# A hybrid decoder step on one core: the gated recurrence goes tile by tile, the first tile ahead of the shared block and the other three inside it

## What is computed

```python
mod = silu(c) @ w_ada + b_ada                    # shift, scale, gate, twice
z = (x * (1 + scale1) + shift1) @ w_in           # 8004 columns, split among the branches
logf = log(lb + (1 - lb) * sigmoid(fa))          # lb from lb_param
# branch A, 8 heads, state S of 128x128, in chunks of 32 tokens (4 for the samples):
bcum = cumsum(logf); k = -expm1(logf)
qe, ke, kd = silu(qa) * exp(bcum), k * exp(-bcum), k * exp(bcum[last] - bcum)
o = qe @ S + mask(qe @ ke.T) @ v                 # v = ia
S = exp(bcum[last]) * S + kd.T @ v
oa = o * rsqrt(mean(o**2) + 1e-6) * a_gnorm * silu(ga)
# branch B: indexer -> top-k keys -> grouped attention with a T5 bias -> ob
x = LN1(ALPHA * x + gate1 * ((sigmoid(gate_a) * oa + sigmoid(gate_b) * ob) @ w_out))
x = LN2(ALPHA * x + gate2 * PEER(x * (1 + scale2) + shift2))   # 8 heads x 16 experts a token
```

## Time and profile before

| | |
|---|---|
| median of three executions | 2604.06 us |
| the profiled execution's own time | 2610.84 us |
| its span, first to last instruction | 2608.9 us |
| mean granted TensorE clock | 0.829 |
| busy: TensorE, VectorE, ACT, POOL | 1945.3, 1459.8, 578.5, 655.6 us |
| moved by DMA | 794.7 MB, mean 305 GB/s |
| stages 1 and 2, stage 3, beat -1, beats 0 to 272 | 393, 222, 202, 1792 us (about) |

### The profile page before, as it was taken

The page is one execution under the profiler, slowest core; times in us unless marked ns, Lnnn a source line. Parts: engine busy times, 40 slices in busy tenths (PEclk is TensorE's granted clock), DMA queues, the critical chain, the costliest instruction groups (busy, mean ns, idle before and its releaser), DMA issues.

```text
span 2608.9 us, 26429 instructions
## 1 busy us (share of the span) xinstructions
PE 1945.3 (75%) x8372; PEld 1048.6 (40%) x8372; DVE 1459.8 (56%) x2984; ACT 578.5 (22%) x1902; POOL 655.6 (25%) x610
## 2 busy tenths in 40 slices
PE   4999994885898986975567756577646667979666
PEld 1878532554664433441243422234311223536311
DVE  1000107563472536689856899747954997353654
ACT  1000002111013544212422223312221113121221
POOL 0000003220002233323333333333433323332342
PEclk8999996675799998787789977889867778695779
DMA  8357301123657989999999999999999999999797
GB/s 315 124 184 279 126 20 50 43 69 124 186 169 279 387 321 371 413 385 361 344 398 420 394 415 374 355 374 418 403 368 346 394 385 409 404 405 366 285 421 301
DMA packets 203327, 794.69 MB, mean 305 GB/s; under 512 B 24435, under 2 KB 87763, under 8 KB 130230
## 3 DMA queue, kind: packets, MB, share of 16 engines
q0 software_dynamic: 81280, 589.48, 56.6%
q1 hardware_dynamic: 116358, 185.59, 20.7%
q10 hardware_dynamic: 5552, 17.94, 2.3%
HBM read 771.24 MB, written 23.91 MB: 305 GB/s over the span
## 4 chain that ended last, share of the span: by engine, by line
PE 25%; DMA 20%; DVE 18%; issue 9%; SPq 3%; ACT 1%; POOL 0%; ACTq 0%; another core or an unknown queue 0%; DVEq 0%; POOLq 0%
DMA uv<-in_peer_uv,eidr 14%; PE PS L1249 9%; PE PS L1296 7%; PE PS L1367 4%; DVE uv L1656 3%; DVE m L1686 2%; DMA uv<-in_peer_uv,eids 2%; DVE sels L1687 2%; SPq L1155 1%; PE PS L1319 1%; PE PS L1419 1%; DMA vec<-mod_d 1%; PE PS L1334 1%; DMA qbt<-mix_d 1%; SPq L1149 1%
## 5 line engine op out<-in xcount | busy, mean ns | idle before, releaser
L1249 PE MATMUL PS<-uv,dg 128*32 128x512 f32 x2176 | 731.3, 753 | 397.0 <-ACT dg L1512 362.9
L1656 DVE CUSTOM_DVE_ANT_0 uv<-uv,h2r 128x1024 f32<-128x1024 f32 x544 | 666.8, 1226 | 416.0 <-DMA uv<-in_peer_uv,eidr 326.9
L1216 POOL DMA_INDIRECT uv<-in_peer_uv,eidr x512 | 552.6, 1079 | 1366.8 <-PE PS L1249 1037.3
L1249 PEld LDWEIGHTS PS<-uv,dg 128*32 128x32 f32 x2176 | 193.4, 127 | 799.3 <-ACT dg L1512 496.4
L1500 ACT ACTIVATE acts<-dots 128x2 f32<-128x2 f32 x272 | 55.3, 203 | 1085.5 <-DVE dots L1656 1048.9
L1367 PEld LDWEIGHTS PS<-h2T,wr 128*128 128x128 f32 x1280 | 178.2, 223 | 63.7 <-issue 60.1
L1367 PE MATMUL PS<-h2T,wr 128*128 128x128 f32 (+1 forms) x1280 | 189.5, 308 | 1.1 <-ACT h2T L1586 1.1
L1296 PE MATMUL PS<-htb,wr 128*128 128x416 f32 x512 | 186.5, 520 | 0.0
L417 PE MATMUL PS<-hT,wb 128*128 128x272 f32 (+1 forms) x608 | 143.7, 398 | 14.4 <-PEq L134 14.4
L1512 ACT ACTIVATE dg<-fold,wts 128x32 f32<-128x32 f32 x544 | 140.9, 306 | 0.0
L417 PEld LDWEIGHTS PS<-hT,wb 128*128 128x128 f32 (+1 forms) x608 | 114.5, 189 | 46.2 <-issue 20.8
(11 more groups left out here) (281 smaller groups left out, 2066.6 us busy)
## 6 DMA issues: line engine op xcount, KB each, us to landing
wr<-in_w_oq SPq DMA_DIRECT2D x120, 512.0 KB
wb<-in_w_in SPq DMA_DIRECT2D x15, 2048.0 KB, 10.2
w_ada_p<-in_w_ada POOLq DMA_DIRECT2D x16, 1024.0 KB, 8.1
wr<-in_w_late SPq DMA_DIRECT2D x32, 512.0 KB
w_ada_b<-in_w_ada SPq DMA_DIRECT2D x8, 1024.0 KB, 20.7
h2r<-h_d ACTq DMA_DIRECT2D x32, 256.0 KB
uv<-in_peer_uv,eidr POOLq DMA_INDIRECT x512
kvr<-in_cache_kt SPq DMA_DIRECT2D x48, 128.0 KB
```

Source lines behind the costliest of these rows:

```text
L1216: nc.gpsimd.indirect_dma_start(out=uv[j % RING][:, :], out_offset=None, in_=table, in_offset=bass.IndirectOffsetOnAxis(ids, 0)).then_inc(e ...
L1249: mm = nc.tensor.matmul(PS[ST * g:ST * g + ST, at:at + 512], dg[:, j % DR, :], uv[j % RING][:, D + 512 * half:D + 512 * half + 512], start ...
L1656: c.step(nc.vector.tensor_tensor_reduce(out=uv[j % RING][:, 0:D], in0=uv[j % RING][:, 0:D], in1=h2r[:, q // HT % 2, g % 2, :], scale=1.0, ...
```

## The change

The recurrence is written once as a set of functions (`recurrence`) over a half of the heads (four) and one tile of 128 tokens, with buffers of 24 KB per partition. Stage 3 does only tile 0, as two halves, and the sample. It spills q, the gate and v of tiles 1 to 3 to memory (rec_d, recv_d) and the states after tile 0 (carry_d). In the shared block each tile has two halves of six steps, ("rec", n, k), put from beats 0, 42 and 96 on at 1.2 a beat: 0 ACT loads (inputs, states and a mask), 1 logarithms, scan and scaling, 2 scores and transposes, 3 products and state steps, 4 outputs, states stored, squares, 5 mean square, inverse root, norm. The result is written straight into mgt, which SP no longer loads for tiles 1 to 3. Their buffers lie over the attention's (tile 1 from selp on, tiles 2 and 3 from gbt on), so that late weights use three of the six ring buffers in these beats, and tile 1's indexer and top-k start at beat 10 instead of 0. The products of a chunk are taken from the 32 rows of the chunk, four narrow ones per head in place of one wide one with a zeroed operand; vc and POOL's work for it are gone. The sample's elementwise work is done for all heads at once. The parameters (lbm, gn, eps6, cmask, meanm) are loaded and computed in stage 1. Shortened, the diff is:

```diff
@@ stage 1
+            for j in range(2):
+                pool.dma_start(lbp[:, j, :], dap(a["lb_param"], j * D, [[1, P], [P, H]]), ...).then_inc(m_lbd, 16)
+            act.wait_ge(m_sm, 1)
+            nc.scalar.activation(lbm[:, 0:2, :], lbp[:, :, :], ACT.Exp).then_inc(m_lb, 1)
@@ stage 3
+        def exponents(act, n):
+            b = buf(n)
+            act.wait_ge(r["scan"], n + 1)
+            nc.scalar.activation(b.eb[:, :], b.bc[:, :], ACT.Exp).then_inc(r["exp"], 1)
+            nc.scalar.activation(b.ke[:, :], b.bc[:, :], ACT.Exp, scale=-1.0).then_inc(r["exp"], 1)
+            act.wait_ge(r["d"], n + 1)
+            nc.scalar.activation(b.ab[:, :], b.ab[:, :], ACT.Exp).then_inc(r["ed"], 1)
...
+        def states(dve, c, n, k):
+            b = buf(n)
+            dve.wait_ge(r["ds"], 4 * n + k + 1)
+            for i in range(4):
...
+                    c.step(nc.vector.scalar_tensor_tensor(b.st[k + 1][:, i, :], b.st[k][:, i, :], b.eb[:, at:at + 1], ds, ALU.mult, ALU.add), done)
...
+        def products(pe, n, first=0, end=4):
+            b = buf(n)
+            for k in range(first, end):
+                lo = CH * k
...
+                for i in range(4):
+                    last = nc.tensor.matmul(bank(banks(n)[k % 2], P, P, P * i), b.kd[lo:lo + CH, i, :], b.v[lo:lo + CH, P * i:P * i + P],
+                                            start=True, stop=True)
+                last.then_inc(r["ds"], 1)
...
-                    nc.tensor.matmul(bank(2 + t % 2), kd_t[:, h % 2, t, :], vc[:, t, :, :], start=True, stop=True).then_inc(r_ds, 1)
...
+            for t in range(1, TILES):
+                for j, src in enumerate((q_s, sn_s)):
+                    sp.dma_start(dap(rec_d, (2 * (t - 1) + j) * P * H * P, [[H * P, P], [P, H], [1, P]]), src[:, :, P * t:P * t + P]).then_inc(r_spill, 16)
+                sp.dma_start(dap(recv_d, (t - 1) * P * D, [[D, P], [1, D]]), v_s[:, t, :]).then_inc(r_spill, 16)
@@ TensorE's order in stage 3
+            rec.scores(pe, 0)
+            rec.scores(pe, 1)
+            rec.products(pe, 0, 0, 2)
+            ... (scores and transposes of the sample)
+            rec.products(pe, 0, 2, 4)
+            rec.products(pe, 1)
+            ... (outputs, mean squares; states and outputs of the sample, head by head)
@@ shared block, the beats
-    for t, b in ((1, 0), (2, 52), (3, 106)):
+    for t, b in ((1, 10), (2, 52), (3, 106)):
         ix, tp, ys, qs = tile_steps(t)
+        put(b - 10, 1.2, *[("rec", n, k) for n in (2 * t - 2, 2 * t - 1) for k in range(6)])
...
-        nxt = (nxt + 1) % WRING
+        nxt = (nxt + 1) % (WRING if n < len(early_w) or piece[0] != "late" else WRING // 2)
@@ SP
-                mixed(mgt[:, :, :], 0, t, z_ga)
+                if t == 0:
+                    mixed(mgt[:, :, :], 0, t, z_ga)
...
+                    if 1 <= t < TILES:
+                        sp.wait_ge(r["mg"], 2 * t)
+                        sp.wait_ge(r_cst, 16 * 2 * t)
@@ ACT
+            def recur(n, k):
+                t, g, b = rec_tile(n), n % 2, rec_buf(n)
+                if k == 0:
+                    if n >= 1:
+                        act.wait_ge(r["mg"], n)
+                        act.wait_ge(r_cst, 16 * n)
...
+                    if g == 0:
+                        act.dma_start(b.keep[:, :], dap(a["keep"], 0, [[N, P], [1, 512]])).then_inc(r_ld, 16)
+                    for j, dst in enumerate((b.q, b.sn)):
+                        act.dma_start(dst, dap(rec_d, (2 * (t - 1) + j) * P * H * P + 512 * g, [[H * P, P], [1, 512]])).then_inc(r_ld, 16)
+                    act.dma_start(b.v, dap(recv_d, (t - 1) * P * D + 512 * g, [[D, P], [1, 512]])).then_inc(r_ld, 16)
+                    act.dma_start(b.st[0][:, :, :], dap(carry_d, 512 * g, [[H * P, P], [1, 512]])).then_inc(r_ld, 16)
+                elif k == 1:
+                    act.wait_ge(r_ld, ld_at(n))
+                    rec.logs(act, n)
+                    rec.exponents(act, n)
...
@@ VectorE
+                if kind == "rec" and k == 1:
+                    dve.wait_ge(r_ld, ld_at(t))
+                    rec.decay(dve, c, t)
+                    rec.scaled(dve, c, t)
+                elif kind == "rec" and k == 2:
+                    rec.masked(dve, c, t)
+                elif kind == "rec" and k == 3:
+                    for i in range(4):
+                        rec.states(dve, c, t, i)
+                elif kind == "rec" and k == 5:
...
+                    rec.normed(dve, c, t)
@@ TensorE
+                elif kind == "rec" and k == 2:
...
+                    rec.scores(pe, t)
+                elif kind == "rec" and k == 3:
+                    rec.products(pe, t)
+                elif kind == "rec" and k == 4:
+                    rec.outputs(pe, t)
+                elif kind == "rec" and k == 5:
+                    rec.mean_squares(pe, t)
```

More of the change, by code:

```diff
@@ L12 @@
 import math
+from dataclasses import dataclass
 from contextlib import ExitStack
@@ new lines, in _ @@
+            last.then_inc(q_ln, 1)
+            rec.exponents(act, 0)
+            rec.exponents(act, 1)
+            act.wait_ge(q_scan, 1)
+            nc.scalar.activation(ebS[:, :], bcS[:, :], ACT.Exp).then_inc(q_exp, 1)
+            nc.scalar.activation(keS[:, :], bcS[:, :], ACT.Exp, scale=-1.0).then_inc(q_exp, 1)
+            act.wait_ge(q_d, 1)
+            nc.scalar.activation(abS[:, :], abS[:, :], ACT.Exp).then_inc(q_ed, 1)
+            rec.keys_out(act, 0)
+            rec.keys_out(act, 1)
@@ new lines, in _ @@
+            act.wait_ge(q_kdp, 1)
+            nc.scalar.activation(kdS[:, :, :], PS[0:ST, 512 * 5:512 * 7].rearrange("p (h k) -> p h k", k=P), ACT.Copy).then_inc(q_kdt, 1)
+            for n in range(2):
+                rec.squares(act, n)
+                rec.inverse_root(act, n)
+            act.wait_ge(q_o, H)
+            nc.scalar.activation(bcS[:, :], bank(7, H * ST), ACT.Square).then_inc(q_sq, 1)
+            act.wait_ge(q_ms, 1)
+            nc.scalar.activation(keS[:, :], bank(7, H * ST, P, 256), ACT.Ln, bias=eps6[:, 0:1]).then_inc(q_lnms, 1)
@@ L630, in _ @@
+            act.wait_ge(q_lnms, 1)
+            nc.scalar.activation(keS[:, :], keS[:, :], ACT.Exp, scale=-0.5).then_inc(q_rstd, 1)
         @block.vector
@@ new lines, in _ @@
+            for i in range(4):
+                rec.states(dve, c, 0, i)
+            dve.wait_ge(q_kdp, 1)
+            c.step(nc.vector.tensor_tensor(by_head(scmS[:, :]), by_head(bank(4, H * ST, ST)), smask[:, :].unsqueeze(1).to_broadcast([ST, H, ST]), ALU.mult), q_scm)
+            for i in range(4):
+                rec.states(dve, c, 1, i)
+            for h in range(H):
+                sample(h)
+                if h in (1, 3):
+                    rec.normed(dve, c, h // 2)
+            dve.wait_ge(q_rstd, 1)
@@ L766, in _ @@
                                             start=False, stop=b == NB - 1)
-                last.then_inc(r_o, 1)
-            mean_squares(H - 1)
+                last.then_inc(q_o, 1)
+            rec.outputs(pe, 0)
+            sample_states(0)
+            sample_outputs(0)
+            rec.mean_squares(pe, 0)
+            rec.outputs(pe, 1)
+            sample_states(1)
+            sample_outputs(1)
+            rec.mean_squares(pe, 1)
+            for h in range(2, H):
+                sample_states(h)
+                sample_outputs(h)
@@ L868, in program @@
     x1 = zu("x1", [P, D])
+    assert zu_at[0] - where["z"] - rest == REC_BYTES
     h2 = zu("h2", [P, D])
@@ L875, in program @@
     assert zu_at[0] <= where["z"] + 65536
+    assert where["z"] + 65536 - at_selp >= REC_BYTES
+    late_half = [rec_buffers("e1", at_selp)]
+    rest_half = [rec_buffers("e2", where["z"] + rest)]
+    keep_of = {1: late_half[0].keep, 2: rest_half[0].keep}
     zb, zb_at = over("z", rest)
@@ L1035, in program @@
                 if kind in ("y", "late") or kind == "query" and k < 2 * PH]
+    early_w = [s for s in beats[-1] if s[0] in ("y", "late") or s[0] == "query" and s[2] < 2 * PH]
     use_at, slot_at, nth_at, before = {}, {}, {}, {}
@@ L1038, in program @@
     for n, piece in enumerate(pieces_w):
[L1039 removed]
+        if piece[0] == "y" and piece[2] == 0 or n == len(early_w):
             nxt = 0
```

533 lines of the change are left out of this document (301 added, 232 removed).

## The result

The changed kernel takes 2676.26 us (median of 4 runs, 2670.14 to 2678.89), the kernel before 2608.16 in the same session. The ratio is 1.0265, 95% interval 1.0235 to 1.0296: slower by 68 us.

What follows compares the result with a forecast made beforehand. TensorE and VectorE alternate in the stage; the block is bound by TensorE for 18 beats, then gathers, with VectorE second. -128 + 72 + 49 + 55 = +48 on 2604 gave 2652 us, range 2555 to 2700.

Steps and rivals of the forecast that it cites:

- The stage, -128: Recurrence stage ahead of the block: without three tiles it takes 94 us against 221.6, saving 128 us (110 to 140).
- C: Tile 1 and stage: TensorE's clock falls to 1.2 GHz after waits, costing 20 and 18 us; 2690 us, chance 0.12.
- D: Recurrence stage: hardly shorter, 130 us, because sample products are short and many; saving 92, total 2688 us, chance 0.07.
- Parameters in stage 1, at nothing: First stage: takes over some 5 us of parameter arithmetic at no cost, up to 15 us if a load lands late.
- Tile 1, +72: Beats 0 to 10, on TensorE's path: waits 52, work 27, less some 7 us of present idle, adding 72 us.
- Tiles 2 and 3, +49 and +55: Beats 42 to 52 and 96 to 106, VectorE's path: work and waits, less 15 us won back each, plus traffic.
- Rival B: Loads in the block are short, 6.5 and 5.2 us instead of 15 and 12: +2, 2606 us, chance 0.17.
- At nothing: Shared block: three weight slots, tile 1's later index and top-k, SP's new waits and carry stores cost nothing.
- The rule on the queues: ACT's loads in the block: 94 or 75 GB/s by trace, though round-robin might let two busy queues share evenly.
- The rule on table switches: ACT in the six halves: 1.28 us per table load by trace; 2.66 with a drain would add 33 us.
- What would show it: Stage 85 to 105 us, beats 0 to 18 some 210, six load waits of 10 or more, DMA share under 0.8.
- Ring covers stalls (A): Shared block: the gather ring absorbs every stall, three tiles cost 39 us: -89, 2515 us, chance 0.17.

Runs made afterwards that it cites:

- experiment 1: The changed kernel without the recurrence of tiles 1 to 3, tile 0's result stored in its place, so only the shorter stage counts: 2509.66 us, ratio 0.9618.
- the run with far loads: The changed kernel with tiles 2 and 3 loading four beats ahead of the first logarithm, other steps one a beat: 2633.82 us, ratio 1.0094.
- the run with the slack beats: The changed kernel with tiles 2 and 3 moved to beats 27 to 42 and 71 to 89, loads four beats ahead: 2627.8 us, ratio 1.0071.
- experiment 4's last schedule: The changed kernel with all three tiles' steps spread, tiles 2 and 3 in less busy beats, and hand-overs further apart: 2606.37 us, ratio 0.9994.

## Why the prediction was right, and where it was wrong

It said 2652 us, 2555 to 2700, slower. 2676 came. The sign holds, and of the mechanism the part that the loads stall three engines in a row. The sum was +48; the medians differ by +68, the profiled executions by +59. That the two are near is in part luck: the stage saved 34 us less than in the sum (at beat 0), the three stretches cost 8 us more, and 30 us came back in beats for which the sum had no term. Of these 11 are the index steps', and 12 go with the granted clock in beats 236 to 246, which no run ties to the change (below).

**The stage, -128, measured -99** (-94 at beat 0). This is the step that failed, and its size is in two terms. The sample's products were costed at the durations of the kernel before, where the clock was 0.70 on the mean and most of them ran at the higher level: the median value product took 587 ns there and 1056 after, the median state product 253 and 354. At 0.50 the value products measured 30.2 us instead of 16.2 and the state products 28.6 instead of 18.8 (groups above): 24 of the 28 us that the stage is longer than the sum's 94.6. The term of 54 us, from the first output product (432.03) to ScalarE's last square, measured 77.4. Outputs began 36 us after the start, not 32, which is the rest. Rivals C and D named this, one as a cooling clock and one as many short products; D's own bound, a stage of 130 us, was nearer the truth than my 94. I had written "it is less if TensorE stays at half clock" and priced it at 18 us at most. No row showed the clock of such a stage without the wide products; I took the old mean over.

**Parameters in stage 1, at nothing:** +2.4 us, inside the 15 allowed.

**Tile 1, +72:** beats 0 to 18 measured +71.9, but by experiment 1 12 us of that are the later index steps, of which beats 18 to 28 give 11 back; the recurrence costs 59. That the number fits is luck. The two loads took 19.8 and 7.3 us where 15 and 12 were assumed, the same sum. Against the kernel with the stage alone (windows above) TensorE's own work in beats 0 to 18 is 28.7 us more (166.7 against 138.0), 27 assumed, and its idle time 31.0 more (46.7 against 15.7), where 52 of waits less 7 had made 45. So the waits were sized 14 us too long.

**Tiles 2 and 3, +49 and +55:** +53.9 and +58.1. The net fits, the two terms don't. Gross I had 64 and 70. The load of a first half is longer than assumed (23.5 and 18.3 us against 15), that of a second far shorter (3.9 and 4.0 against 12). So I had taken a rate from the nearest load and applied it to all; by the windows around tile 2's two loads it goes by how much is queued beside it: a full ring at the first load, less at the second. Rival B, the short load, is right for the second halves alone. And the 15 us that each tile should win back afterwards from the full ring came to nothing: beats 72 to 82 took 67.4 us, against 67.7 before, 52 to 62 and 106 to 116 the same 62.4 and 67.2. That step was wrong as to where. If the ring's lead is won back at all, it is inside the stalled beats, between one stall and the next, which no run separates.

**At nothing:** three slots and the later index steps, +1.5 us over beats 0 to 28 in the kernel with the stage alone. Right as a sum. Beats 236 to 246, which the change doesn't touch, took 84.3 us instead of 96.6; in the ten other runs they took from 80.8 to 97.2. They go with the granted clock: 0.61 in the two profiles of 96.6 and 97.2 us (before, and the run with far loads), 0.64 to 0.67 in those of 84 to 90, 0.70 at 80.9, and in each the length is TensorE's busy time (80.4 us before, 68.3 after) and 16 us. Why the clock differs there is left open; I couldn't tie it to an edit.

**The rule on the queues.** The prediction set 94 and 75 GB/s beside a share of the queues. Tile 2's first load, 1.31 MB, took 25.3 us, from 1084.4 to 1109.7, or 52 GB/s of 412: about an eighth of what moved, beside some 9 MB of gathers and weights. An even share between two queues, which was my own reading of the round-robin and not the section's words, is not what came.
**The rule on table switches.** The logarithm ends at 1054.39, the table load starts at 1054.41, and the exponent follows it at 1055.70 (timeline of the run with the slack beats). No drain is seen there, so the term of 33 us finds no support.

**What would show it:** the waits for the load above 10 us are three, not six, and two (3.9 and 4.0 us) are under the 7 us that I had named as a sign of being wrong, so for the second halves of tiles 2 and 3 the load stall isn't there; beats 0 to 18 reached 213 us (210 forecast); the DMA share 0.67 and 0.66 where under 0.8 was forecast; the stage 122.5 us, outside 85 to 105.

**Ring covers stalls (A):** refuted as a whole, three tiles cost 166 us. But experiment 4's last schedule shows what it would take: loads four beats ahead, hand-overs one or two beats apart, and 70 us are covered. What isn't then: 14 us of traffic, TensorE's queue in beats 0 to 18 (TensorE 167.3 of 199.0 us busy), and the relay where VectorE has no room.

## What to carry to other kernels

Moving work from a stage where two engines alternate into a block bound by transfers can pay only if each step of it comes up in its engine's queue when its input is there; here the best order tried reached the time of the kernel before and no less. Count, for each step, how long the engines before it take, and put that many beats between; issue its loads by their time under load, here four beats, not in the beat of their use. And don't price a stage that is left over at the mean clock of the old one. That the wide products that went had kept the mean up fits the rows, but no run shows it by itself.

## What the runs showed that I had not expected

- TensorE without any idle time in the profile for 70 us, nearly all of it on products with 32 rows by 512 columns or 128 rows by 4, 32 and 128 columns (the halves' mean squares, 128 rows by 512, are among them and don't lift it), has a granted clock of 0.50 in all of it; the kernel before, busy 156.3 of 221.6 us, had 0.70. Wide products of 128 rows raise it to 1.00 while they run (395 to 410 us), and mixing two of 256 columns into each head doesn't. Which property of the products decides was not tried.
- A load of 1.3 MB beside a full gather queue takes nearly as long as the queue: it landed after 25.3 us and 10.6 MB, with 1.7 MB still to come. Where the ring isn't full, ScalarE's wait for the load of 1 MB is 4 us. By this a longer ring would make such loads slower; that was not tried.
- Seven megabytes more in a block whose DMA share is 0.99 cost 14 us. Taking 50 us of ScalarE's load waits away brought at most some 9 us where another wait stood behind (two beats ahead), and 42 us in all where none did (four beats ahead).
